# Whole-row loads, a rearranged first round and gap, and key squares summed in two rounded parts, in a hybrid decoder layer

## The reference, cut to what matters

```python
h = rmsnorm(x, g_mix_pre)
proj = jnp.einsum('bld,de->ble', h, w_in)
...
qkv, buf_b_new = causal_dwconv(jnp.concatenate([bq, bk, bv], axis=-1), buf_b, b_conv_w, None)
qb, kb, vb = jnp.split(jax.nn.silu(qkv), 3, axis=-1)
kb = l2norm(kb.reshape(Bn, L, B_HEADS, B_DK))      # x * rsqrt(sum(x*x) + eps)
ob, S_b_new = gated_delta_chunked(qb, kb, vb, gdec, beta, S_b.astype(f32))
...
mix = jnp.einsum('ble,ed->bld', jnp.concatenate([oa, ob, oc], axis=-1), w_out)
x = x + rmsnorm(mix, g_mix_post).astype(x.dtype)
h2 = rmsnorm(x, g_ffn_pre)
ff = jnp.einsum('blf,fd->bld', jax.nn.silu(h2 @ w_gate) * (h2 @ w_up), w_down)
```

## Time and profile before

| | |
|---|---|
| median of 3 runs (lowest, highest) | 1352.7 us (1351.7, 1353.6) |
| the profiled execution | 1352.5 us |
| its span, first to last instruction | 1350.7 us |
| PE, PEld busy | 1336.2 us, 1306.7 us |
| DVE, ACT, POOL busy | 838.9 us, 684.4 us, 72.6 us |
| transfers | 234 MB, mean 173 GB/s |
| chain that ended last | PE 92%, DVE 4%, ACT 2% |

### The profile page before, as it was taken

How to read it: one execution, slowest core, us unless ns; L and a number is a source line. 1 busy time by engine, 2 the same in 40 slices (tenths; PEclk the granted TensorE clock), 3 DMA queues, 4 the chain that set the end, 5 groups by cost and what they waited for, 6 DMA issues and landing times.

```text
span 1350.7 us, 28088 instructions
## 1 busy us (share of the span) xinstructions
PE 1336.2 (99%) x11361; PEld 1306.7 (97%) x11361; DVE 838.9 (62%) x1197; ACT 684.4 (51%) x980; POOL 72.6 (5%) x155
## 2 busy tenths in 40 slices
PE   8999999999999999999999999999999999999998
PEld 7998989899999999899999999999999999999998
DVE  7788787876979875586555555555555544444443
ACT  6665656564847665555434444344344434434343
POOL 3110101010200001100000000000000000000000
PEclk9999999999999999999999999999999999999999
DMA  7463636364756555455665555655555555555552
GB/s 245 142 189 111 207 111 206 112 205 125 231 156 188 159 164 186 146 187 169 176 185 177 181 184 177 182 180 178 186 177 180 184 175 187 175 185 180 180 183 85
DMA packets 225670, 234.08 MB, mean 173 GB/s; under 512 B 10483, under 2 KB 220694, under 8 KB 225580
## 3 DMA queue, kind: packets, MB, share of 16 engines
q1 hardware_dynamic: 220916, 218.86, 52.5%
q0 software_dynamic: 4672, 14.04, 3.5%
HBM read 223.45 MB, written 9.65 MB: 173 GB/s over the span
## 4 chain that ended last, share of the span: by engine, by line
PE 92%; DVE 4%; ACT 2%; issue 1%; DMA 1%; SPq 0%; ACTq 0%; DVEq 0%
PE ps L655 27%; PE ps L656 27%; PE ps L657 27%; PE ps L722 2%; PE ps L982 1%; DVE conv L1926 1%; DVE w_lo L1750 1%; PE ps L799 1%; ACT w_hi L1238 1%; DMA xtok<-in_x_prompt_dram 1%; PE ps L1203 0%; PE ps L864 0%; PE ps L886 0%; PE ps L834 0%; PE ps L892 0%
## 5 line engine op out<-in xcount | busy, mean ns | idle before, releaser
L1750 DVE TENSOR_TENSOR w_lo<-raw,w_hi 128x1024 fp32r<-128x1024 f32 x408 | 499.5, 1226 | 419.7 <-ACT w_hi L1238 419.4
L1238 ACT ACTIVATE w_hi<-raw 128x1024 fp32r<-128x1024 f32 x408 | 430.7, 1058 | 537.7 <-PE ps L657 528.9
L655 PE MATMUL ps<-act_hi,w_hi 128*128 128x264 f32 x2232 | 644.5, 289 | 1.3 <-DVE w_lo L1750 1.3
L656 PE MATMUL ps<-act_lo,w_hi 128*128 128x264 f32 x2232 | 633.3, 284 | 0.0
L657 PE MATMUL ps<-act_hi,w_lo 128*128 128x264 f32 x2232 | 632.4, 283 | 0.0
L655 PEld LDWEIGHTS ps<-act_hi,w_hi 128*128 128x128 f32 x2232 | 420.1, 188 | 7.8 <-issue 5.0
L656 PEld LDWEIGHTS ps<-act_lo,w_hi 128*128 128x128 f32 x2232 | 420.5, 188 | 1.2
L657 PEld LDWEIGHTS ps<-act_hi,w_lo 128*128 128x128 f32 x2232 | 419.3, 188 | 0.0
L656 PE MATMUL ps<-hid_lo,w_hi 128*128 128x264 f32 x696 | 197.8, 284 | 0.0
L655 PE MATMUL ps<-hid_hi,w_hi 128*128 128x264 f32 x696 | 197.7, 284 | 0.0
L657 PE MATMUL ps<-hid_hi,w_lo 128*128 128x264 f32 x696 | 197.6, 284 | 0.0
(11 more groups left out here) (415 smaller groups left out, 1079.6 us busy)
## 6 DMA issues: line engine op xcount, KB each, us to landing
raw<-in_w_in_dram SPq DMA_DIRECT2D x112, 512.0 KB, 3.7
raw<-in_w_gate_dram SPq DMA_DIRECT2D x88, 512.0 KB, 3.5
raw<-in_w_up_dram SPq DMA_DIRECT2D x88, 512.0 KB, 3.5
raw<-in_w_down_dram SPq DMA_DIRECT2D x88, 512.0 KB, 3.5
raw<-in_w_out_dram SPq DMA_DIRECT2D x32, 512.0 KB, 3.5
out_dram<-Ss POOLq DMA_DIRECT2D x12, 512.0 KB, 5.3
Ss<-in_state_gdn_dram POOLq DMA_DIRECT2D x8, 512.0 KB, 7.3
xtok<-in_x_prompt_dram SPq DMA_DIRECT2D x4, 512.0 KB, 6.2
```

What stands on the lines that cost most here:

```text
L655: pe.matmul(out, wh, x_hi[:, kk], start=(kk == begin), stop=False)
L656: pe.matmul(out, wh, x_lo[:, kk], start=False, stop=False)
L1238: return act.activation(out, in_, f, **kw)
L1750: tt(w_lo[:, slot], raw[:, slot], w_hi[:, slot].bitcast(F32), sub).then_inc(lo_done, 1)
```

## The change

The prompt's two blocks of 128 rows are loaded and squared whole, in two transfers instead of four; the sample rows' sum, Ln and Exp come between the two; one `keep_busy` of the opening less stands between the transposes, another is gone ahead of `spread_norm`. In round 0 DVE's gate table and the convolutions stand at other positions. The key squares of rounds 1 to 4 are made twice by ACT, in full and in rounded format; DVE subtracts; PE sums both parts in products of rounded format. The tails' transposes move behind the output projection, their copies from DVE to ACT, and ACT's table load one chunk ahead.

```diff
-                for h in range(2):
-                    cols = slice(h * D // 2, (h + 1) * D // 2)
-                    sp.dma_start(xtok[t][:, cols], x_prompt[0, t * P:(t + 1) * P, cols]).then_inc(x_in[t][h], 16)
+                sp.dma_start(xtok[t][:, :], x_prompt[0, t * P:(t + 1) * P, :]).then_inc(x_in[t], 16)
...
             def b_step(hp, n):
                 if hp == 1:
-                    pe.wait_ge(mx["sq"], 2 * n + 1)
+                    pe.wait_ge(mx["sq"], 3 * n + 2)
+                    pe.wait_ge(mx["osq"], 3 * n + 1)
...
                     for i in range(2):
-                        last = pe.matmul(ps[:, 4 + i, 0:T], ones[:, :], sq[:, i], start=True, stop=True)
+                        pe.matmul(ps[:, 4 + i, 0:T], ones[:, :].bitcast(F32R), sq_hi[:, i], start=True, stop=False)
+                        last = pe.matmul(ps[:, 4 + i, 0:T], ones[:, :].bitcast(F32R), sq_lo[:, i], start=False, stop=True)
...
             keep_busy(1, 0, 2)
             turn_sample_rows()
-            turn_raw(0, 0)
             keep_busy(1, 0, 2)
-            turn_raw(0, 1)
+            turn_raw(0)
+            sample_sum()
             keep_busy(1, 0, 2)
-            turn_raw(1, 0)
-            pe.wait_ge(raw_cp, 2)
-            keep_busy(1, FILL_BANK, 2)
-            turn_raw(1, 1)
-            sample_sum()
+            pe.wait_ge(raw_cp, 1)
+            pe.wait_ge(x_ss, 2)
+            turn_raw(1)
             turn_gains()
-            keep_busy(1, FILL_BANK, 2)
             spread_norm()
...
-                if g == 4:
-                    turn_tails()
             product_sum()
-            keep_busy(3, 5, 2)
+            turn_tails()
+            keep_busy(2, 5, 2)
...
             act.wait_ge(pool_c, 4)
...
+            row_squares(0)
+            act.wait_ge(n_pe, 2)
+            A(norm_mv[:, L:T], ps[:, SUM_BANK, 0:NB], ACT.Ln, scale=1.0 / D, bias=eps).then_inc(x_ss, 1)
+            act.wait_ge(x_ss, 2)
             A(norm_mv[:, L:T], norm_mv[:, L:T], ACT.Exp, scale=-0.5, bias=first_row).then_inc(x_ss, 1)
+            row_squares(1)
+            act.wait_ge(x_ss, 4)
+            A(xss[:, 1, 0:2], xss[:, 0, 0:2], ACT.Ln, scale=1.0 / D, bias=eps).then_inc(x_ss, 1)
+            act.wait_ge(x_ss, 5)
+            A(xss[:, 3, 0:2], xss[:, 1, 0:2], ACT.Exp, scale=-0.5).then_inc(x_ss, 1)
...
                     A(sq[:, 0:2], qkv[:, 1], ACT.Square).then_inc(mx["sq"], 1)
+                    A(sq_hi[:, :, :], qkv[:, 1], ACT.Square).then_inc(mx["sq"], 1)
                     A(nrm[:, 0], qkv[:, 0], ACT.Square).then_inc(mx["sq"], 1)
...
+                if pos == 29:
+                    ln_exp_tables()
...
             g = OUT_GROUPS - 1
-            ln_exp_tables()
...
+                if q == 0:
+                    act.wait_ge(tl_pe, 1)
+                    for i, n in enumerate((72, 120, 72, 80)):
+                        A(rows[0:n, i, :], ps[0:n, 6, i * P:i * P + P]).then_inc(tl_cp, 1)
...
                 if pos == 0:
+
+                    dve.wait_ge(mx["sq"], 3 * n + 2)
+                    tt(sq_lo[:, :, :], sq[:, 0:2], sq_hi[:, :, :].bitcast(F32), sub).then_inc(mx["osq"], 1)
...
+                if pos == 11:
+                    taps(1, 1, 2)
+                if pos == 13:
+                    taps(2, 1, 2)
+                lo_at(pos)
                 if pos == 7:
                     gating()
-                if pos == 11:
+                if pos == 8:
+                    taps(0, 1, CONVW)
+                if pos == 9:
                     gating_table()
                     table_columns()
+                if pos == 11:
+                    taps(1, 2, CONVW)
+                if pos == 13:
+                    taps(2, 2, CONVW)
```

More of the change, by code:

```diff
@@ L76 @@
 OPEN_C = 8
-SS_BANK, SS_COL, PAR_BANK, RBC_BANK, FILL_BANK, GATE_BANK = 3, 256, 6, 5, 4, 5
-S_DONE, COPIED = 11, 13
+SS_BANK, SUM_BANK, PAR_BANK, RBC_BANK, GATE_BANK = 3, 1, 6, 5, 5
+S_DONE, COPIED = 3, 8
 SERIES = [1 / 15, 1 / 13, 1 / 11, 1 / 9, 1 / 7, 1 / 5, 1 / 3, 1.0]
@@ L169, in hybrid_layer @@
         YT = sqv[:, 768:896].rearrange("p (r t) -> p r t", r=4)
+        sq_lo = put("sq_lo", [P, 2, T], F32R, offset=place["sq"])
+        sq_hi = put("sq_hi", [P, 2, T], F32R, offset=place["sq"] + 8 * T)
         fold = sqv[:, 768:1024].rearrange("p (x t) -> p x t", x=4)
@@ L254, in hybrid_layer @@
         silu_done = sem("silu_done")
-        x_in = [[sem(f"x_in{t}{h}") for h in range(2)] for t in range(2)]
+        x_in = [sem(f"x_in{t}") for t in range(2)]
         xs_in = sem("xs_in")
@@ L675, in _, with turn_raw @@
             pe.wait_ge(pool_c, 8)
-            def turn_raw(t, h):
-                pe.wait_ge(x_in[t][h], 16)
-                for q in (2 * h, 2 * h + 1):
+            def turn_raw(t):
+                pe.wait_ge(x_in[t], 16)
+                for q in range(4):
                     bank = q + 4 if t == 0 else q
@@ L692, in sample_sum @@
                 pe.wait_ge(n_dve, 2)
-                pe.wait_ge(raw_cp, 4)
-                pe.matmul(ps[:, PAR_BANK, SS_COL:SS_COL + NB], ones[:, :], oT[:, 1, 0:NB], start=True, stop=True)\
+                pe.matmul(ps[:, SUM_BANK, 0:NB], ones[:, :], oT[:, 1, 0:NB], start=True, stop=True)\
                     .then_inc(n_pe, 1)
@@ L699, in turn_gains @@
                 pe.wait_ge(par0_in, 6 * 16)
+                pe.wait_ge(raw_cp, 4)
                 pe.transpose(ps[:, PAR_BANK, 0:112], stage[0:112, 0], ident[0:112, 0:112]).then_inc(n_pe, 1)
@@ L942, in out_sum @@
                 if not isinstance(n, int) or n < B_ROUNDS:
-                    pe.wait_ge(mx["osq"], 2 * n + 2)
+                    pe.wait_ge(mx["osq"], 3 * n + 3)
                 else:
-                    pe.wait_ge(mx["osq"], n + B_ROUNDS + 1)
+                    pe.wait_ge(mx["osq"], n + 2 * B_ROUNDS + 1)
                 pe.wait_ge(mx["s2"], 2 * n + 2)
@@ L1170, in _ @@
                         pe.wait_ge(o_r, 1)
+                    else:
+                        pe.wait_ge(tl_cp, 4)
                 if s == 0:
@@ L1252, in _ @@
             ln_exp_tables()
[L1253 to L1263, removed]
@@ L1265, in _ @@
-            act.wait_ge(pool_c, 4)
[L1266 to L1279, removed]
-            A(norm_mv[:, L:T], norm_mv[:, L:T], ACT.Exp, scale=-0.5, bias=first_row).then_inc(x_ss, 1)
+            def row_squares(t):
+                act.wait_ge(x_in[t], 16)
+                A(hF[:, :, :].rearrange("p k t -> p (k t)")[:, t * D:t * D + D], xtok[t][:, :], ACT.Square,
+                  accum_out=xss[:, 0, t:t + 1]).then_inc(x_ss, 1)
@@ L1281, in _ @@
+            act.wait_ge(x_ss, 5)
+            A(xss[:, 3, 0:2], xss[:, 1, 0:2], ACT.Exp, scale=-0.5).then_inc(x_ss, 1)
             for q in range(4):
                 split(q // 2, 2 * q % RING, first=q < 2)
+                if q == 0:
+                    act.wait_ge(gain_in, 1)
                 for k in range(4 * q, 4 * q + 4):
@@ L1778, in _ @@
             dve.tensor_copy(params[:, 0:112], ps[:, PAR_BANK, 0:112]).then_inc(gain_in, 1)
-            raw_copy(1, 1)
-            dve.wait_ge(x_ss, 9)
+            dve.wait_ge(x_ss, 6)
             for t in range(2):
                 tsc(norm_mv[:, t * P:t * P + P], ident, xss[:, 3, t:t + 1], None, mul).then_inc(n_dve, 1)
+            raw_copy(1, 1)
             dve.wait_ge(n_pe, 4)
@@ L2063, in b_step @@
                 if pos == 14:
-                    dve.wait_ge(mx["osq"], 2 * n + 1)
-                    dve.wait_ge(mx["sq"], 2 * n + 2)
+                    dve.wait_ge(mx["osq"], 3 * n + 2)
+                    dve.wait_ge(mx["sq"], 3 * n + 3)
                     stt(sq[:, 0:2], nrm[:, 0], Q_SCALE, sq[:, 0:2], mul, add).then_inc(mx["osq"], 1)
@@ L2216, in _, with lo_at, taps @@
             parameters()
+            def lo_at(pos):
+                lo(pos + AHEAD, (pos + AHEAD) % RING)
+            def taps(i, first, end):
+                convolve(i, i % 2, 0, taps=range(first, end))
             for pos in range(OPEN_C - AHEAD, SLOTS):
@@ L2229, in _ @@
                     tsc(upper[:, :], upper[:, :], 1.0, 200.0, sub, mul)
-                if pos in (10, 11, 12):
-                    chained[0] = TAPS * (pos - 10)
-                    convolve(pos - 10, pos % 2, 0, taps=range(1, CONVW))
             dve.wait_ge(st_act, 12)
@@ L2305, in _ @@
                     add_squares(0, pos // 4 - 1)
-                if pos == 22:
-                    dve.wait_ge(tl_pe, 1)
-                    for i, n in enumerate((72, 120, 72, 80)):
-                        dve.tensor_copy(rows[0:n, i, :], ps[0:n, 6, i * P:i * P + P]).then_inc(tl_cp, 1)
             fold_squares(0)
```

2 lines of the change are left out of this document (1 added, 1 removed).

## The result

The changed kernel takes 1358.7 us (median of six runs, 1357.0 to 1362.0) against 1352.5 for the kernel before (six runs): a ratio of 1.005, interval 1.0039 to 1.006. The prediction was 1358.1, in a range of 1355.6 to 1361.4. The number came out; the working behind it did so only in part. Two effects were missed by over a microsecond each, in opposite directions: the opening, and TensorE's clock. That they nearly cancel is luck.

A forecast was written before the change was run, and what follows sets the result against it. PE, busy 99% of the span, was taken to bound the kernel through its instruction stream and few waits. Terms 0.39 + 0.80 + 4.80 - 0.61 = +5.38 took the median from 1352.7 to 1358.1 us, range 1355.6 to 1361.4.

The forecast's parts named there:

- Rounds 2 to 4, +4.80: Key sums: PE waits 2.01 us for DVE's late subtraction, less 0.41 gained, so 1.60 lost in each of three rounds.
- The gain of 0.41: Key sums, per round: four rounded products at 0.12 us each, 0.48 in all, replace full-format sums costing 0.89.
- Start of round 1: Wait for w_lo gone (-1.44), new wait for the subtraction at the key sum (+2.65), cheaper sums (-0.41): +0.80 us.
- Gap, -0.61: Between output projection and feed-forward: tail transposes leave the output stage (-0.44), DVE's last sum starts sooner (-0.17).
- Opening, +0.39: Before the first weight product: squaring a whole row takes longer, so norm_mv and all that follows come 0.39 us later.
- if the data land when they do now: Opening: assumption that the prompt's last data arrive no sooner than before, on which the +0.39 us rests.
- the bound of -0.2: Opening: other bound of the term, should the data come 0.6 us sooner.
- the prediction's own sign for a wrong term: Opening: a first weight product starting before 15.4 would show the term wrong; near 16.0 was expected.
- Rival (a): New waits send PE's clock to half: one stretch gives 1359.7, four give 1364.5; chance 0.20.
- Rival (b): DVE is not late at the key sum: -3.30 us, so 1349.4, faster; chance 0.06.
- Rival (c): Opening gains: data 0.6 us sooner and first products at full clock, 1355.9, or 1355.1 with two waits shorter; chance 0.10.
- half-clock stretch: PE's clock at half after a stop, as in the opening: at most 4 x 0.41 = 1.6 us each.

The follow-up runs named there:

- e2: The changed kernel with 22 (round 1) or 16 (rounds 2 to 4) unread products on PE ahead of the wait at the key sum: 1356.9 us.
- e1: The changed kernel with the full-format key sums of before, no second Square and no subtraction; opening, round 0 and gap stay changed: 1350.1 us.
- e5: The changed kernel with both key Squares ahead of Ln and Exp of the output's norm and the subtraction ahead of finish, for round 1 inside round 0: 1348.5 us.
- e6: The kernel before with only the second Square, subtraction and rounded key sums added; opening, round 0 and gap as before: 1362.3 us.
- e4: The changed kernel with the prompt again in four transfers of half rows, the rest of its opening waiting for whole rows: 1360.2 us.

## Why the prediction was right, and where it was not

- **Rounds 2 to 4, +4.80: right, a little small.** With the clock effect out of the way (e2) the three rounds grew by 1.61, 1.81 and 1.81, 5.23 in all. The chain from output sum to key sum was worked out as 7.26 us; it is 7.16 in round 2, and 7.35 and 7.33 in rounds 3 and 4. The earlier trace rows were read at the end of round 1; at the ends of rounds 2 and 3 DVE stands idle for 0.18 ahead of the cast in `finish`, which those rows can't show. The gain of 0.41 on the four rounded sums, taken from the big products' pace, is 0.39 (e1 against e5). The 0.18 could have been read in the trace of the kernel before, at the end of round 2:

```profile
208.59 0.43 DVE L2108 CAST cat_hi<-oT 128x528 f32 x1 [0.18 <-DVE oT L2106]
```

- **Start of round 1, -1.44 + 2.65 - 0.41 = +0.80: right.** e2 grew by 0.84 there. The wait for `w_lo` is gone, and the wait at the key sum is 2.80 (71.79 + 0.12 to 74.71), where 2.65 was given. Only the sentence that the gain is eaten one chunk later misleads: without the new order of round 0 the sum waits 2.42 all the same (e6), so most of that gain stays.
- **Gap, -0.61: right**, measured -0.63. The tails' copies on ACT are covered.
- **Opening, +0.39: wrong in sign.** The step that failed is "if the data land when they do now", with the bound of -0.2 behind it. The work behind the landing did get longer, from 15.59 - 10.9 = 4.7 to 14.55 - 9.4 = 5.15, so by 0.46 where 0.39 was predicted. But the data landed 1.5 us sooner. The prediction credited the two issues that SP saves to the weights' loads only, though the second row stands behind the same issues, and took the pace of the quarters in the earlier trace rows as the rate at which data arrive. The result is -1.04 at the first weight product, and its start at 14.55 meets the prediction's own sign for a wrong term, a start before 15.4.
- **Rival (a), half clock behind the waits: it came in part.** It had a chance of 0.20 beside a forecast without it. Five of the changed kernel's six runs have some of it, with a mean granted clock of 0.994 to 0.997. The opening's -1.34, the rounds' +0.43 and the clock's +1.8 in the median run nearly cancel, so that forecast and result lie 0.6 apart by luck. Without the clock the terms should have given 1356.9, the time of e2.
- **Rival (b)** fell with the first timeline: DVE is late. **Rival (c)** had the direction of the opening right (data 0.6 sooner were given, it was 1.5) and the rest wrong: the half clock in the opening stayed, from 16.04 to 19.46.
- A half-clock stretch was priced at 1.6 us. In round 3 it cost 1.50 (3.31 less e2's 1.81), in round 1, twice as long, 2.77. Ahead of the feed-forward, 575.83 to 579.24, only 0.75, because part of it fell on waits that PE had there anyway.

## What to carry to other kernels

A cheaper form of an operation whose input needs one more step on another engine can cost more than it saves: look at where that step stands in that engine's list and what the engine does ahead of it. Here three instructions of a round, moved a few places (e5), turned +6 us into -4 with the same work. Of a transfer that work waits for, count the issues ahead of it on its queue's engine: here two issues fewer were worth 0.9 us, and larger transfers nothing that could be seen.

## What the runs showed of the hardware

- Waits of 1.9 to 2.8 us of PE, each with a busy PE on both sides, were followed by half clock at some places and not at others: in the profiled run behind the waits of 2.8 (round 1) and 2.1 (round 3), not behind those of 1.9 (round 2) and 2.1 (round 4). Ahead of the feed-forward the same stop of 1.68 us between two products had half clock behind it in this run and none in the profile of before. With the waits filled by products none came behind the opening in the profiled run, and all five runs had a mean clock of 0.998 or more; of the fifteen runs of the three kernels with the four waits open (the changed one, e4, e6) thirteen had 0.997 or less. The trace of e4, with the same four waits, has half clock from 214.36 to 217.77 and from 286.04 to 289.45, behind those of rounds 3 and 4, and none behind the longest, 2.8 in round 1, where its key sum starts at 75.39:

```profile
72.00:80.00 8.00, 5.36 (x43) 5.05 (x42) 5.68 (x10) 7.10 (x10) 1.95 (x4) 1.00 0.96 275
```

- These waits are not needed for it: the kernel without them (e5) has three of eleven runs at 1350.5 to 1350.7 with a mean clock of 0.996, and of the 49 runs of the kernel before that stood beside these experiments eight lie at 1353.4 or more, with 0.997. Both kernels keep shorter stops, the 1.68 us ahead of the feed-forward among them, and none of these runs has a trace, so whether half clock comes without any stop is not shown. What decides it in a given run was not found.
- The Trainium skill (TensorE: Matmul & The Clock Gate, section on HAM oscillation) has PE's stops between bursts of work bring the half clock back; the stops of its example are longer than these. e2 against the changed kernel bears it out as a tendency; stops of equal length with different outcomes, as above, show that the length of one stop does not decide it alone.
